# Two norms of the rows from one pass of squares, taken beside the last feed-forward, in a two-model transformer kernel on one Trainium2 core

## The reference

```python
def rmsnorm(x, g):
    return x * lax.rsqrt(jnp.mean(x * x, axis=-1, keepdims=True) + EPS) * g

x = first_block(x, ...)      # ends with: x = x + (silu(g) * u) @ w_down[1]; return rmsnorm(x, final_norm)

def second_block(x, c, ctx, ...):
    h_lat = modulate(x, norm_g[0, 0], sh1, sc1)      # rmsnorm_2(x, g) * (1 + scale) + shift
    h_ctx = modulate(ctx, norm_g[0, 0], csh1, csc1)
    y_ctx, y_lat = mixer_ab(h_ctx, h_lat, ...)       # h @ w_in, recurrences, norm of heads, gate, @ w_out
```

## Time and profile before

| | |
|---|---|
| median of 3 runs | 3202.28 us |
| the profiled execution | 3200.67 us |
| its span | 3198.7 us |
| PE matmul busy | 3109.7 us, 97% |
| DVE, ACT, POOL busy | 1816.1, 1181.0, 1239.4 us |
| mean granted clock of PE | 0.985 |

### The profile page before, as it was taken

How to read it: one execution, slowest core, us unless ns; L and a number is a source line. 1 busy time by engine, 2 the same in 40 slices (tenths; PEclk the granted TensorE clock), 3 DMA queues, 4 the chain that set the end, 5 groups by cost and what they waited for, 6 DMA issues and landing times.

```text
span 3198.7 us, 41807 instructions
## 1 busy us (share of the span) xinstructions
PE 3109.7 (97%) x16548; PEld 2561.7 (80%) x16548; DVE 1816.1 (57%) x2931; ACT 1181.0 (37%) x1851; POOL 1239.4 (39%) x568
## 2 busy tenths in 40 slices
PE   8999999999999999998998999999999999999998
PEld 7658888886589888777888998778888777878887
DVE  3556787845553664674336877466786448362223
ACT  4543222235544333234336654342223435432222
POOL 4304444433166344333434554234444320134442
PEclk9999999999999999998999999899999999999999
DMA  7204554522145223222333343335653210123331
GB/s 128 76 14 125 174 153 142 177 63 76 44 126 150 87 74 92 72 66 93 112 106 96 110 117 116 106 107 170 190 156 117 86 57 10 40 66 103 96 92 66
DMA packets 480435, 323.89 MB, mean 101 GB/s; under 512 B 102521, under 2 KB 447745, under 8 KB 479729
## 3 DMA queue, kind: packets, MB, share of 16 engines
q1 hardware_dynamic: 475472, 309.60, 33.1%
q10 hardware_dynamic: 2656, 6.30, 0.5%
q0 software_dynamic: 2112, 5.32, 0.5%
HBM read 315.90 MB, written 5.24 MB: 100 GB/s over the span
## 4 chain that ended last, share of the span: by engine, by line
PE 86%; DVE 8%; ACT 3%; issue 1%; POOL 1%; DMA 0%; DVEq 0%; ACTq 0%; POOLq 0%
PE G L2715 13%; PE G L2724 12%; PE G L2725 12%; PE G L2729 12%; PE G L2940 6%; PE G L2941 6%; PE G L2945 6%; PE G L2740 3%; PE G L3798 1%; PE G L3155 1%; POOL WL L727 1%; PE S L3822 1%; PE S L3068 1%; ACT WH L786 1%; PE G L3094 1%
## 5 line engine op out<-in xcount | busy, mean ns | idle before, releaser
L727 POOL TENSOR_TENSOR WL<-raw,WH 128x1024 fp32r<-128x1024 f32 (+1 forms) x520 | 1216.6, 2361 | 1852.6 <-ACT WH L786 1852.6
L786 ACT ACTIVATE WH<-raw 128x1024 fp32r<-128x1024 f32 (+1 forms) x520 | 492.3, 995 | 609.2 <-PE G L2945 426.3
L2724 PE MATMUL G<-hH,WH 128*128 128x512 f32 x1520 | 595.7, 392 | 0.0
L2725 PE MATMUL G<-hL,WH 128*128 128x512 f32 x1520 | 592.6, 390 | 0.0
L2729 PE MATMUL G<-hH,WL 128*128 128x512 f32 x1520 | 360.1, 389 | 0.0
L2724 PEld LDWEIGHTS G<-hH,WH 128*128 128x128 f32 x1520 | 285.9, 188 | 60.9 <-ACT t_s L1246 0.8
L2725 PEld LDWEIGHTS G<-hL,WH 128*128 128x128 f32 x1520 | 285.8, 188 | 58.8
L2729 PEld LDWEIGHTS G<-hH,WL 128*128 128x128 f32 x1520 | 285.3, 188 | 59.2
L1615 DVE SCALAR_TENSOR_TENSOR acc<-adaw,cvec,acc 128x512 f32<-128x512 f32 x280 | 251.7, 951 | 4.2
L2715 PE MATMUL G<-hH,WH 128*128 128x512 f32 (+1 forms) x432 | 166.9, 386 | 2.8 <-POOL WL L727 2.8
L2715 PE MATMUL G<-hH,WL 128*128 128x512 f32 (+1 forms) x432 | 164.3, 380 | 0.0
(11 more groups left out here) (732 smaller groups left out, 6222.1 us busy)
## 6 DMA issues: line engine op xcount, KB each, us to landing
raw<-ffn_w_in_in SPq DMA_DIRECT2D x264, 256.0 KB, 3.4
adaw<-ada_w_in SPq DMA_DIRECT2D x48, 1024.0 KB, 5.3
raw<-ab_w_in_in SPq DMA_DIRECT2D x128, 256.0 KB, 3.0
raw<-ffn_w_out_in SPq DMA_DIRECT2D x96, 256.0 KB, 2.9
raw<-w_gate_in SPq DMA_DIRECT2D x88, 256.0 KB, 3.3
raw<-w_up_in SPq DMA_DIRECT2D x88, 256.0 KB, 3.4
raw<-w_down_in SPq DMA_DIRECT2D x64, 256.0 KB, 2.9
raw<-w_in_in SPq DMA_DIRECT2D x40, 256.0 KB, 3.7
```

What stands on the lines that cost most here:

```text
L727: nc.gpsimd.tensor_tensor(WL[c % 2][:, cut], raw[c % 2][:, cut], WH[c % 2][:, cut].bitcast(F32), ALU.subtract)\
L786: nc.scalar.activation(WH[c % 2][:, cut], raw[c % 2][:, cut], ACT.Copy).then_inc(weights_hi, 1)
L2724: mm(dst, view(WH[c % 2], k), high, start=(k == 0 and not (joint and i)), stop=False)
L2725: mm(dst, view(WH[c % 2], k), low, start=False, stop=False)
```

## The change

The squares of the last feed-forward's result are taken as soon as each part is final, with `final_square` on ACT: once plain, for the final norm, and once with the factor `g_final`, for the latent's norm. Parts 0 and 1 are squared after the root of the context's heads, parts 2 to 5 one step of the generator later, parts 6 and 7 between the high parts `c.m.H1`, `H2` and `H3`. DVE adds both kinds in `final_add`, parts 1 to 6. PE sums both in one place after c.o3, into eight columns of M[0]. The second statistic is then worked out on 4 columns: `fin.rec2` = rec * rec, `t.n1.var` = sum * rec2, its root on ACT (`final_roots`, now after c.o3's eviction and the chunk work behind it), its reciprocal. Both broadcasts stand after c.o4, into M[0] and M[1]. The context's transposes stand after c.o5 (first half) and c.o7 (second half). The separate statistics of t.n1 and their `keep_busy` products are gone, also the eight ahead of the opening. On ACT the weight chunk that was made after c.o7 (the latent's second, t.ab + 1) is now made inside the opening, between `t.n1.H1` and `t.n1.H2`; the copies of the context's second half stand behind `t.n1.H7`.

```diff
--- before.py
+++ after.py
@@ -345,6 +345,7 @@
                 cs1, self.st1, _ = lay(part, f("cs1", N // P + 1, 2 * P), f("st1", N))
                 self.ob, _ = lay(part + size([P, HA, N]), f("ob", HA, N))
                 self.y, _ = lay(PT_.last, f("y", KD, N))
+                assert e - size([P, N // P, 4 * P]) == ctxend + 24 * 1024
                 self.rs, _ = lay(e - size([P, N // P, 4 * P]), f("rs", KD, N))
 
                 self.b1, self.k1, states = lay(rows, f("b1", HA, N), f("k1", HA, N))
@@ -366,6 +367,7 @@
 
         PT_ = Latent()
         PC = ContextPass()
+        gained, _ = lay(ctxend + 24 * 1024, ("gained", [P, 4, T], F32))
         ctxT, _ = lay(PT_.part, ("ctxT", [P, KD, TC], F32))
         ra_wk, rb_em, _ = lay(arena, ("ra_wk", [P, T], F32), ("rb_em", [P, T], F32))
         held = {"ra": ra_wk[0:64, :], "wk": ra_wk[64:128, :], "rb": rb_em[0:64, :], "em": rb_em[64:128, :], "wi": PT_.bg[0:64, :],
@@ -1120,14 +1122,35 @@
                     nc.scalar.activation(ps.rs[:, k, :], o, ACT.Square).then_inc(act_done, did("act", f"c.hs{k}"))
                 yield
                 root("c.h", KD * ps.sc, P, S[0])
-                stats_before[0] = "c.h.sum"
-                yield
+                for k in range(2):
+                    final_square(k)
+                yield
+                for k in range(2, 6):
+                    final_square(k)
                 yield
                 for k in range(KD):
                     act.wait_ge(dve_done, at("dve", f"c.h{k}"))
                     if k == 0:
                         act.wait_ge(pe_done, at("pe", f"b1.up{FT - 1}"))
                     nc.scalar.activation(hH[:, k, 0:N], ht[:, k % 2, 0:N], ACT.Copy).then_inc(act_done, did("act", f"c.m.H{k}"))
+                    if k in (1, 2):
+                        final_square(5 + k)
+
+            def final_square(k):
+
+                act.wait_ge(dve_done, at("dve", f"b1.down3.{k}"))
+                if k >= 3:
+                    act.wait_ge(dve_done, at("dve", f"fin.adB{k - 2}"))
+                nc.scalar.activation(sq[:, k % 2, :] if k else rstd[:, :], xT[:, k, :], ACT.Square).then_inc(act_done, did("act", f"fin.sqA{k}"))
+                nc.scalar.activation(gained[:, 1 + k % 2 if k else 0, :], xT[:, k, :], ACT.Square, scale=g_final[:, k:k + 1])\
+                    .then_inc(act_done, did("act", f"fin.sqB{k}"))
+
+            def final_roots():
+
+                root("fin", T // P, D)
+                act.wait_ge(dve_done, at("dve", "t.n1.var"))
+                nc.scalar.activation(ncol[:, 12:16], ncol[:, 12:16], ACT.Sqrt, bias=eps[:, 0:1], scale=1.0 / D).then_inc(act_done, did("act", "t.n1.root"))
+                root_before[0] = "t.n1.bc"
 
             def joint_high(q):
 
@@ -1413,7 +1436,7 @@
                     nc.scalar.activation(y[:, k, :], G[k % 4][:, 0:N], ACT.Copy).then_inc(act_done, did("act", f"{n}.y{k}"))
                     if n != "c":
                         added_square(f"{n}.y1", k, y[:, k, :], lambda k: act.wait_ge(act_done, at("act", f"{n}.y{k}")))
-                    if k % 2 and (n == "c" or k < KD - 1):
+                    if k % 2 and k < KD - 1:
                         hi(c + 2 + k // 2)
                     for at_k, then in after:
                         if at_k == k:
@@ -1451,14 +1474,10 @@
                 ended(n, ps.y2, N, 2)
 
 
-            for k in range(KD):
-                added_square("fin", k, xT[:, k, :], lambda k: act.wait_ge(dve_done, at("dve", f"b1.down3.{k}")))
             stats_before[0] = "fin.sum"
-            projected("c", PC.y, TC, KD, ((1, lambda: root("fin", T // P, D)),))
-            turned_context(2)
+            projected("c", PC.y, TC, KD, ((3, final_roots), (5, lambda: turned_context(2))))
+            rounded("t.n1", KD, hH, f"c.o{KD - 1}", T, shift("t", 0), late=first["t.ab"] + 1)
             turned_context(3)
-            stats("t.n1", KD, lambda k: xT[:, k, :], lambda k: act.wait_ge(dve_done, at("dve", f"fin.{k}")))
-            rounded("t.n1", KD, hH, f"c.o{KD - 1}", T, shift("t", 0))
             act.dma_start(scratch[0], xT[:, :, :].rearrange("p k t -> p (k t)")).then_inc(x_out, 16)
             latent_columns()
             context_feed_forward(latent_recurrence())
@@ -2164,7 +2183,10 @@
                 dve.wait_ge(act_done, at("act", "c.h.root"))
                 dve.wait_ge(dve_done, here())
                 own(V.reciprocal(ncol[:, 0:KD * nsc], S[0][:, 0:KD * nsc]), "h.rec")
-                yield
+                final_add(1)
+                yield
+                for k in range(2, 6):
+                    final_add(k)
                 yield
 
                 def rest(k):
@@ -2194,12 +2216,28 @@
             columns("c", range(4))
             columns("t", range(4))
             first_mixing(1)
+            def final_add(k):
+
+                dve.wait_ge(act_done, at("act", f"fin.sqB{k}"))
+                if k > 1:
+                    dve.wait_ge(dve_done, at("dve", f"fin.adB{k - 1}"))
+                V.tensor_tensor(rstd[:, :], rstd[:, :], sq[:, k % 2, :], ALU.add).then_inc(dve_done, did("dve", f"fin.adA{k}"))
+                V.tensor_tensor(gained[:, 0, :], gained[:, 0, :], gained[:, 1 + k % 2, :], ALU.add).then_inc(dve_done, did("dve", f"fin.adB{k}"))
+
             context_columns()
             feed_forward("b1", xT, T, FH1, FL1, silu1, False, context_recurrence())
 
-            mean("fin")
+            final_add(6)
+            roots("fin")
+            dve.wait_ge(dve_done, here())
+            V.tensor_tensor(ncol[:, 8:12], ncol[:, 0:4], ncol[:, 0:4], ALU.mult).then_inc(dve_done, did("dve", "fin.rec2"))
+            dve.wait_ge(dve_done, here())
+            V.tensor_tensor(ncol[:, 12:16], M[0][:, 4:8], ncol[:, 8:12], ALU.mult).then_inc(dve_done, did("dve", "t.n1.var"))
+            dve.wait_ge(act_done, at("act", "t.n1.root"))
+            V.reciprocal(ncol[:, 4:8], ncol[:, 12:16]).then_inc(dve_done, did("dve", "t.n1.rec"))
+            dve.wait_ge(pe_done, at("pe", "fin.bc"))
             for k in range(KD):
-                V.scalar_tensor_tensor(xT[:, k, :], xT[:, k, :], g_final[:, k:k + 1], M[1][:, :], ALU.mult, ALU.mult)\
+                V.scalar_tensor_tensor(xT[:, k, :], xT[:, k, :], g_final[:, k:k + 1], M[0][:, :], ALU.mult, ALU.mult)\
                     .then_inc(dve_done, did("dve", f"fin.{k}"))
 
             def added(n, which, y, x, g, N):
@@ -2600,7 +2638,7 @@
                     V.scalar_tensor_tensor(kc[:, g, :], kc[:, g, :], g_qk[:, 1:2], M[1][:, g * TC:g * TC + TC], ALU.mult, ALU.mult)\
                         .then_inc(dve_done, did("dve", f"k.kn{g}"))
 
-            mean("t.n1")
+            dve.wait_ge(pe_done, at("pe", "t.n1.bc"))
             normed("t.n1", KD, lambda k: xT[:, k, :], gain("t", 0), hH, hL, T, shift("t", 0))
             latent_columns()
             context_feed_forward(latent_recurrence())
@@ -2760,7 +2798,7 @@
 
             stats_before = [None]
 
-            AWAKE = {"b0.n1", "b0.n2", "b1.n1", "t.n1", "t.y1", "t.n2", "t.y2", "m.n1", "m.y1", "m.n2", "m.y2"}
+            AWAKE = {"b0.n1", "b0.n2", "b1.n1", "t.y1", "t.n2", "t.y2", "m.n1", "m.y1", "m.n2", "m.y2"}
 
             def keep_busy(n, times):
 
@@ -3688,19 +3726,32 @@
                 if n != "m":
                     stats(f"{n}.y2", KD, N)
 
-            def context_again():
+            def context_again(half):
 
                 pe.wait_ge(ctx_loaded, 32)
-                turned_context(2, ctxin2)
-                turned_context(3, ctxin2)
+                turned_context(half, ctxin2)
 
             def final_sums():
 
                 pe.wait_ge(dve_done, at("dve", f"c.h{KD - 1}"))
-                feature_sums("fin", KD)
-
-            project_out("c", TC, ((3, final_sums), (5, lambda: spread_roots("fin")), (7, context_again)))
-            stats("t.n1", KD)
+                pe.wait_ge(dve_done, at("dve", f"fin.adB{KD - 2}"))
+                for i, total in enumerate((rstd, gained[:, 0, :])):
+                    for t in range(4):
+                        mm(M[0][:, 4 * i + t:4 * i + t + 1], total[:, t * P:t * P + P], ones[:, 0:1], start=(i == 0 and t == 0), stop=False)
+                pe.wait_ge(act_done, at("act", f"fin.sqB{KD - 1}"))
+                for i, last_square in enumerate((sq[:, 1, :], gained[:, 2, :])):
+                    for t in range(4):
+                        last = mm(M[0][:, 4 * i + t:4 * i + t + 1], last_square[:, t * P:t * P + P], ones[:, 0:1], start=False, stop=(i == 1 and t == 3))
+                last.then_inc(pe_done, did("pe", "fin.sum"))
+
+            def final_spread():
+
+                pe.wait_ge(dve_done, at("dve", "t.n1.rec"))
+                to_all(M[0][:, :], 0).then_inc(pe_done, did("pe", "fin.bc"))
+                to_all(M[1][:, :], 4).then_inc(pe_done, did("pe", "t.n1.bc"))
+                stats_before[0] = f"fin.{KD - 1}"
+
```

(1 more changed line is left out.)

## The result

The changed kernel takes **3179.62 us** (median of 5 runs, 3176.96 to 3182.11). The kernel before, on the same chip, takes 3198.76 us (3195.06 to 3202.49, 5 runs). The ratio is 0.994, 95% interval 0.9925 to 0.9954: 19 us less, between 15 and 24. The forecast was 3188 with a range of 3183 to 3196, so the sign is right and the size is not.

What follows compares the result with a forecast made beforehand. PE, busy 97% of the span, was taken as the bound. The latent's second chunk at 1497.1 + 11.7 + 1.3 = 1510.1, not 1523.79, saves 13.7 us: 3200.67 becomes 3187.0, 3188.6 by the median, stated as 3188, range 3183 to 3196.

Steps and rivals of the forecast that it cites:

- the joint: From the context's first product to the latent's second chunk: that chunk starts at 1510.1 instead of 1523.79, 13.7 us less.
- The delay ahead: At the context's first product: PE starts 0.2 us late because of the squares and additions, ends 0 and 1.3.
- The ladder of additions: Beside the feed-forward's end: squares and DVE additions, at most 0.78 us per addition, end about 1457.3.
- Rival C: Feed-forward's end: additions of 2.70 us each stop PE, 20 us come in, time 3209; chance 0.03.
- The sums: After c.o3: 32 matmuls take 4.2 us, as the same number over the heads did.
- c.o4: Behind the sums: 24 matmuls at 1.2 GHz, 0.215 us each, take 5.1 us and end at 1483.95.
- The second statistic: After the sums: two roots, reciprocals and products on four columns take 1.5 us or less, hidden behind c.o4.
- The collision in the opening: Latent's first 48 matmuls: low parts 2 and 3 wait for POOL's weight work, 1.3 us later, ends 0 and 3.2.
- the low end: Whole kernel: 3183, the better case's time with 2 us off for a median of three runs spreading over 4.7.
- Rival E: After the sums and in the opening: clock doesn't fall, collision costs nothing; gain 17.2 us, 3185; chance 0.07.
- Rival B: Opening partly at 1.2 GHz: half its matmuls slow lose 4.8 us, 3193; all lose 9.6, 3198; chance 0.15.
- Rival D: Behind the opening: later weights or the second chunk come no earlier, gain given back, 3200 to 3204; chance 0.05.

Runs made afterwards that it cites:

- before again: The kernel before, profiled and timed once more with nothing changed: 3198.03 us, ratio 1.0002.
- e_mix: Changed kernel with the 16 sum calls put between the matmuls of c.o3 instead of in a row behind it: 3179.36 us, ratio 0.9942.
- e_pool: Changed kernel with POOL's low part of the latent's second chunk waiting until the last low part of the latent's norm is done: 3177.98 us, ratio 0.9936.
- e_late: Changed kernel with the latent's second chunk made at its old place, after c.o7's eviction: 3187.45 us, ratio 0.9960.
- e_awake: Kernel before without the products of the identity that keep PE busy around t.n1: 3198.78 us, ratio 1.0001.
- e_sq: Changed kernel with all 16 squares and 12 additions back behind the context's high and low parts: 3191.66 us, ratio 0.9973.
- e_three: Changed kernel with POOL's wait for the eighth low part, sums between c.o3's products, and broadcasts behind c.o5: 3179.60 us, ratio 0.9945.

## Why the prediction was wrong in size and right in kind

The forecast's sum against PE's starts, in us:

| stretch | forecast | before | before again | after |
|---|---|---|---|---|
| context's first product to the sums | 14.1 | 14.08 | 14.08 | 14.09 |
| sums to c.o4 | 4.2 | 4.65 | 4.65 | 3.49 |
| c.o4 to the end of c.o7 | 16.3 | 13.77 | 15.04 | 15.74 |
| end of c.o7 to the opening | 1.9 | 19.89 | 20.59 | 2.12 |
| opening | 13.0 | 11.03 | 11.48 | 14.23 |
| the joint | 49.5 | 63.42 | 65.84 | 49.67 |

**The delay ahead (0.2 us)** was right. The ladder of additions, at 0.69 us each, ended at 1449.2, 3.4 us ahead of the context's first product; the forecast had 3.1. Squares took 0.62 us plain and 0.71 with the gain column. PE's waits at the first two products were 0.40 and 1.56 us, as before. Rival C did not come.

**The sums** took 3.49 us, not 4.2. The row of the head sums, from which 4.2 came, was taken while the clock fell (0.82 over its 4.21 us); these 32 ran at 1.00.

**c.o4** was taken at 1.2 GHz throughout, 5.1 us. It took 4.44, since the slow stretch ended inside it:

```profile
1470.24:1474.68 4.44, 4.44 (x26) 4.44 (x26) 2.67 (x4) 0.54 (x2) 2.79 (x2) 0.62 0.48 136
```

**The second statistic** was costed at 1.5 us or less. It took 3.4, from the first root at 1470.41 to the last reciprocal's end at 1473.79, and was hidden even so, under the 4.44 us of c.o4; 2.9 us at the full clock would have been some 0.7 short. DVE's timeline, then POOL's:

```profile
1470.90 2.15 DVE L2233 TENSOR_TENSOR ncol<-ncol 128x4 f32<-128x4 f32 x1
1473.09 0.16 DVE L2235 TENSOR_TENSOR ncol<-M,ncol 128x4 f32<-128x4 f32 x1
```

```profile
1468.35 4.68 POOL L729 TENSOR_TENSOR WL<-raw,WH 128x1024 fp32r<-128x1024 f32 x2 [1.01 <-ACT WH L788]
```

Bounding these products by "a small instruction" left out with whom they share. The one with both inputs in SBUF took 2.15 us for four columns and ended as POOL's second half did (1473.05 and 1473.03). The one with an input in PSUM took 0.16, but by then POOL had ended; the contrast is shown by e_mix, where it took 0.16 us beside a running POOL instruction (1478.84, POOL from 1478.73 to 1481.09).

**The collision in the opening** was 1.3 us in the forecast, and 2.5 by e_pool. The mechanism is the one named. DVE's timeline, then POOL's:

```profile
1490.33 1.88 DVE L1590 SCALAR_TENSOR_TENSOR hL<-ht,mod,hH 128x512 fp32r<-128x512 f32 x1
...
1492.91 2.09 DVE L1590 SCALAR_TENSOR_TENSOR hL<-ht,mod,hH 128x512 fp32r<-128x512 f32 x1
```

```profile
1488.81 5.64 POOL L729 TENSOR_TENSOR WL<-raw,WH 128x1024 fp32r<-128x1024 f32 x2 [3.08 <-ACT WH L788]
```

These are `t.n1.L2` and `L3`; L3 ended 9.0 us behind c.o7, not 8.0: POOL's pair took 5.64 us instead of the 4.86 of the earlier trace rows, 0.8 more. That other half of the rule in the Trainium skill (SBUF — State Buffer, § Who interferes with whom), by which POOL waits for a DVE instruction that got in first, was weighed at 0.4 us and left out of the sum. The trace agrees with it and makes it twice as large, since both of POOL's instructions met it: they took 2.85 and 2.82 us, against 2.4 for one elsewhere in the trace.

**What failed.** These errors cancel: of the joint of the changed kernel the forecast was 0.2 us off. The step that failed is the value from which the gain was taken: "Against the profiled execution's 3200.67 that is 3187.0; the median of the runs is 1.6 higher, so 3188.6 by it", with the low end's "2 us for the median of three runs", and in the sum itself the "1523.79" that stands for the old joint. The miss is 8.4 us, 3188 less 3179.6.

- 3.5 us: the starting value. The two starts, 3200.67 and 3202.28 (the median of three), gave 3188, that is 13.7 less than 3201.7; 53 executions have 3198.2. From there 13.7 less is 3184.5, inside the range.
- Up to 2.4 us: the old joint. 63.42 was read as a property of the program. It holds stretches of 1.2 GHz behind sums and waits, and the repeat had 65.84 with a clock of 0.84. A clock of 0.84 over 65.84 us is 21 us at half speed, 0.89 over 63.42 is 14, and 0.97 over 49.67 is 3. The change removes the very piece where PE was slow, so the gain is larger whenever that piece is slower.
- The last 2.5 us or more are explained by no run. By all executions of both kernels the gain is 18.2 us (3198.2 less 3180.0), and the traces show 13.75 to 16.2 of it in the joint. The rest is within the interval of the measurement (15 to 24 us), and nothing is claimed of it.

Rival E gave 3185 as the better case, by a clock that doesn't fall and a collision that costs nothing. Neither happened in the changed kernel; what of the extra gain is explained came from the kernel before. Rival B didn't come in the change, but e_late and e_awake show it is real. Rival D did not come: the windows behind the joint are 1674.91 and 1674.77 us.

What stays open is why one execution stands at 1.2 GHz longer than another with the same instructions. No run here tells it.

## What to carry to other kernels

Read the granted clock of the stretch that a change removes, and in more than one execution: a stretch of waits and small matmuls has no fixed length, and what its removal is worth differs as much. A difference between two profiled executions is to be cut at instructions that both have; here a third of it lay where the programs are the same. And a kernel's own spread belongs into the forecast: here 3.4 us per thousandth of mean clock, with a median of three off by 4.

## What the runs showed of the hardware

- A DVE product of 128x4 with both inputs in SBUF took 2.15, 1.67, 1.17 and 1.19 us beside POOL's low part (changed kernel, e_sq, e_mix, e_three). The next one, with one input in PSUM, took 0.16 us in all four; in the last three POOL was running beside it.
- 32 sums of one column took 3.49 us in one block, and behind them stand some 3 us at 1.2 GHz (1470.24 to 1473.64, changed kernel). Between the products of c.o3 they left none (clock 1.00 over 50 us, e_mix).
- A wait of PE of 1.1 us ahead of the opening, and two of 1.2 us inside, left the clock at 1.00 (1488.10 to 1502.33). One of 3.62 us was followed by 6.80 us at 0.50 (e_late).
